# A fused two-block transformer forward on one core: modulation slabs in halves, output slabs split in place, gate order turned

## The reference, cut to what matters

```
mod   = silu(c) @ w_ada + b_ada                    # 6 x 1024 columns, 12 slabs of 512
h     = x * (1 + scale) + shift                    # slabs 0..3 give shift and scale
q, k, v, index, gb, gc, hc = split(h @ w_in)
attn  = softmax(mask_topk(rope(q) @ rope(k).T)) @ v
conv  = gb * short_conv(gc * hc)
mix   = concat(rms(attn), rms(conv)) @ w_out       # w_out: 2 slabs of 512 columns
x     = alpha * x + gate * mix;  then layer norm, SwiGLU, layer norm
```

```
h = h + swiglu(rms_norm(h, norm_ffn))
h = h + sigmoid(rms_norm(h, ple_norm) @ ple_w_gate) * (p @ ple_w_proj)
```

## Time and profile before

| | us |
|---|---|
| median of 3 runs | 1129.81 |
| lowest, highest | 1126.03, 1134.69 |
| the profiled execution | 1127.35 |
| its span in the profile | 1125.6 |

### The profile page before, as it was taken

One profiled execution on the slowest core, in us unless ns is written; L12 is line 12 of the kernel. 1 busy time (PEld: TensorE's weight loads), 2 busy tenths in 40 slices (PEclk: granted clock), 3 DMA queues, 4 the chain that ended last, 5 costly groups with the idle time before them and its releaser, 6 DMA issues.

```text
span 1125.6 us, 20288 instructions
## 1 busy us (share of the span) xinstructions
PE 1064.8 (95%) x7913; PEld 984.5 (87%) x7913; DVE 720.5 (64%) x1127; ACT 554.3 (49%) x954; POOL 223.8 (20%) x248
## 2 busy tenths in 40 slices
PE   5999988999999899989999999979987999999998
PEld 5577677999999698879999999978865899999998
DVE  4785777777645567748565645666768766564554
ACT  2223555544454666327454544655446764544453
POOL 0110002323312121012333311141110133332102
PEclk9999989999999999999999999989998999999999
DMA  9962464577557354404555456644440264645651
GB/s 351 400 266 75 150 237 138 168 248 265 153 157 223 103 205 142 159 1 143 191 191 180 147 155 191 225 150 150 150 150 1 76 225 160 212 133 148 202 191 39
DMA packets 183556, 192.78 MB, mean 171 GB/s; under 512 B 5881, under 2 KB 143394, under 8 KB 183490
## 3 DMA queue, kind: packets, MB, share of 16 engines
q1 hardware_dynamic: 182480, 191.15, 50.3%
q0 software_dynamic: 144, 0.52, 0.2%
q10 hardware_dynamic: 866, 0.21, 0.1%
HBM read 190.83 MB, written 1.05 MB: 170 GB/s over the span
## 4 chain that ended last, share of the span: by engine, by line
PE 56%; DVE 5%; ACT 2%; issue 2%; POOL 1%; POOLq 0%; ACTq 0%
PE gemm L1978 17%; PE gemm L1980 17%; PE gemm L1979 17%; PE aux L2438 1%; DVE wlo L1321 1%; PE aux L2100 1%; PE aux L2502 1%; ACT whi L867 1%; DVE state L1873 1%; PE aux L2496 1%; DVE neg_max L1937 1%; DVE d_p L1953 0%; DVE g_b L1827 0%; PE gemm L2528 0%; ACT ohi L1103 0%
## 5 line engine op out<-in xcount | busy, mean ns | idle before, releaser
L1321 DVE TENSOR_TENSOR wlo<-raw,whi 128x1024 fp32r<-128x1024 f32 (+2 forms) x324 | 369.1, 1184 | 78.7 <-ACT whi L867 78.2
L1978 PE MATMUL gemm<-ohi,whi 128*128 128x256 f32 x1376 | 388.7, 283 | 1.7 <-DVE wlo L1321 1.4
L1979 PE MATMUL gemm<-olo,whi 128*128 128x256 f32 x1376 | 385.6, 280 | 0.0
L1980 PE MATMUL gemm<-ohi,wlo 128*128 128x256 f32 x1376 | 384.5, 279 | 0.0
L867 ACT ACTIVATE whi<-raw 128x1024 fp32r<-128x1024 f32 (+2 forms) x324 | 288.7, 956 | 66.0 <-PE gemm L1980 50.9
L1978 PEld LDWEIGHTS gemm<-ohi,whi 128*128 128x128 f32 x1376 | 259.7, 189 | 5.1 <-issue 2.6
L1979 PEld LDWEIGHTS gemm<-olo,whi 128*128 128x128 f32 x1376 | 259.9, 189 | 0.6 <-issue 0.5
L1980 PEld LDWEIGHTS gemm<-ohi,wlo 128*128 128x128 f32 x1376 | 259.7, 189 | 0.0
L1980 PE MATMUL gemm<-acthi,wlo 128*128 128x256 f32 x528 | 147.8, 280 | 0.0
L1978 PE MATMUL gemm<-acthi,whi 128*128 128x256 f32 x528 | 147.5, 279 | 0.0
L1979 PE MATMUL gemm<-actlo,whi 128*128 128x256 f32 x528 | 147.3, 279 | 0.0
(11 more groups left out here) (351 smaller groups left out, 1509.5 us busy)
## 6 DMA issues: line engine op xcount, KB each, us to landing
raw<-in_ffn_w_in SPq DMA_DIRECT2D x44, 1024.0 KB, 6.2
raw<-in_ffn_w_out SPq DMA_DIRECT2D x32, 704.0 KB, 5.8
part<-in_w_ada SPq DMA_DIRECT2D x32, 512.0 KB, 10.5
raw<-in_gla_w_in SPq DMA_DIRECT2D x6, 2048.0 KB, 7.6
raw<-in_diff_w_in SPq DMA_DIRECT2D x6, 2048.0 KB, 7.6
raw<-in_w_gate SPq DMA_DIRECT2D x11, 1024.0 KB, 6.4
raw<-in_w_up SPq DMA_DIRECT2D x11, 1024.0 KB, 8.6
raw<-in_w_down SPq DMA_DIRECT2D x16, 704.0 KB, 5.4
```

What stands on the lines that cost most here:

```text
L1321: dve.tensor_tensor(wlo[hslot][:, q * w:(q + 1) * w], raw[slot][:, q * w:(q + 1) * w], whi[hslot][:, q * w:(q + 1) * w].bitcast(F32), ALU. ...
L1978: pe.matmul(dst, st_hi, mv_hi, start=start, stop=False)
L1979: pe.matmul(dst, st_hi, mv_lo, start=False, stop=False)
L1980: return pe.matmul(dst, st_lo, mv_hi, start=False, stop=stop_)
```

## The change

The first two modulation slabs leave the ring and come in two halves of four row blocks, each with its own semaphore, and the sums of the second stand on PE ahead of the transposes of x. The two slabs of w_out leave the ring as well: they are loaded into the place of `wlo` (`out_w`), ACT splits them from there, and DVE's low part overwrites them in place. Slab 0 is split beside the in_gc projection and made low ahead of the heads, slab 1 a quarter a head in heads 4 to 7. The modulation parts get ten buffers from the start, two of them are used earlier (parts 8 and 9 ahead of the heads, part 10 before the first maxima), and the list of parts by head ends with single ones. The group norms of attention tiles 0 and 1 move up into heads 6 and 7, and `out_columns` begins with these two row blocks ahead of the last product with v. In the gate projections the sigmoid's table is loaded by a small dummy instruction, the first sigmoid comes after one quarter, the sigmoid of a tile comes ahead of the operands of the tile before, DVE adds ahead of making the low operand, and slab 1's quarters are split one, one, one and one over tiles 0 to 2.

```diff
-    ada = lambda i: Phase(f"ada{i}", 1, SLAB, 0, 1, by="mod", ahead=False, ring=i < 2, slot=i % 2)
+    ada = lambda i: Phase(f"ada{i}", 1, SLAB, 0, 1, by="mod", ahead=False, ring=False, slot=i % 2)
...
-        Phase("out0", 2, SLAB, 4, 1, slot=1), *ffn(0),
+        Phase("out0", 2, SLAB, 4, 1, ring=False, slot=1), *ffn(0),
...
+        out_w = [sb(f"out_w{i}", SLAB, at=place[f"wlo{i}"]) for i in range(2)]
...
-            return (n % 8, n // 8) if n < 16 else (8 + n % 2, (n - 16) // 2)
+            return (n % 10, n // 10) if n < 18 else (8 + n % 2, 1 + (n - 18) // 2)
...
-        DONE_BEFORE = {"gate_up0": 4, "gate_up1": 2, "gate_up2": 2, "diff_q": 2}
+        DONE_BEFORE = {"out0": 4, "gate_up0": 4, "gate_up1": 2, "gate_up2": 2, "diff_q": 2}
...
+            elif first and ph.name in ("ple_gate1", "ple_gate2"):
+                each = (1, 0, 0, 0) if act else (0, 0, 0, 0)
...
+            if at.i == 0 and ph.name in ("ple_gate1", "ple_gate2"):
+                return {0: (1,) if act else (0, 1), 1: (2,), 2: (3,)}.get(t, ())
             return {0: (2,), 1: (3,)}.get(t, ()) if act else {0: (1,), 1: (2,), 2: (3,)}.get(t, ())
...
+            def load_out(i):
+                sp.wait_ge(*((tile_done, PH["in_q"].tile0 + 4), (part_used, 18))[i])
+                sp.dma_start(flat(out_w[i], KT, 512), kmaj(a["w_out"][0], 0, 512, i)).then_inc(out_in[i], 16)
...
             for t in range(4):
                 take("in_gc", t, tl(gc, t), gc_ready)
+                for q in {0: (0, 1), 2: (2, 3)}.get(t, ()):
+                    split(PH["out0"], At(0), q)
...
             def beside_head(i):
-                if i in (5, 6):
-                    act.wait_ge(part_used, 12)
-                    split_all("out0", None, range(2 * i - 10, 2 * i - 8))
                 if i == 5:
-                    group_squares(0, attn_ready, 2)
+                    group_root(0, G[0])
+                if i >= 4:
+                    split(PH["out0"], At(1), i - 4)
                 if i == 6:
-                    group_root(0, G[0])
                     group_squares(2, gated_ready, 2)
+                    high_parts(0, 1)
                 if i == 7:
-                    high_parts(0, 1)
                     group_root(2, G[1])
...
+                act.activation(lam[:, 6:7], eps[:, 0:1], ACT.Sigmoid)
...
+                    if k == 1 and m == KT - 1:
+                        operand(m - 1)
                     act.wait_ge(ple_in, n + 1)
                     wait(act, ple_prod, n - k)
                     act.activation(tl(sg, t % 2), tl(gt, t % 2), ACT.Sigmoid).then_inc(ple_sig, 1)
+                    if k == 1 and 0 < m < KT - 1:
+                        operand(m - 1)
                     for q in quarter_between(ph, at, t, act=True):
                         ahead(ph, at, q)
-                    if k == 1:
-                        act.wait_ge(ple_added, m + 1)
-                        scaled_high_and_square(m, B("norm_mix_2", KT + m), a0, dhi, gsq)
...
-            add_heads(range(0, 4))
             modulate_part(6)
             modulate_part(7)
+            add_heads(range(0, 4))
+            modulate_part(8)
+            modulate_part(9)
             add_heads(range(4, IH))
...
-            PARTS_OF_HEAD = ((8, 9), (10, 11), (12, 13), (14, 15), (16, 17), (18, 19), (20,), (21,))
+            PARTS_OF_HEAD = ((11, 12), (13, 14), (15, 16), (17, 18), (19, 20), (21,), (22,), (23,))
             me.again()
+            for q in range(4):
+                low(PH["out0"], At(0), q)
+            modulate_part(10)
             masked_maxima(0)
             for i in range(NH):
                 invert_sums(i)
                 if i + 1 < NH:
                     masked_maxima(i + 1)
+                if i == 6:
+                    mix_norm(0, 1)
+                if i == 7:
+                    mix_low(0, 1)
                 if i < 4:
                     short_conv(i)
                 else:
                     gated_conv(i - 4)
-                for q in {6: (0, 1), 7: (2, 3)}.get(i, ()):
-                    low(PH["out0"], At(0), q)
-                if i == 7:
-                    mix_norm(0, 1)
+                    low(PH["out0"], At(1), i - 4)
                 for n in PARTS_OF_HEAD[i]:
                     modulate_part(n)
...
                     me.did(dve.tensor_tensor(tl(gt, t % 2), bank[:, 0:T], rstd[:, 0:T], ALU.mult), ple_in)
+                    low_between(ph, at, t)
+                    add(m)
                     if k == 1 and m:
                         rest(m - 1)
-                    low_between(ph, at, t)
-                    add(m)
...
             last_columns(1)
+            first_sums_of(1)
             pe.wait_ge(x_in, 16)
...
-            out_columns(0, range(4), OUT_ORDER[0:4], True, False)
+            out_columns(0, range(4), OUT_ORDER[0:2], True, False)
+            values(NH - 1)
+            group_stats((3, 1), C("blk"), mix_sq, X[0:2])
+            out_columns(0, range(4), OUT_ORDER[2:4], False, False)
```

More of the change, by code:

```diff
@@ L532, in build @@
         sources = {
-            **{f"ada{i}": columns(ada, 512 * ADA_ORDER[i]) for i in range(2)},
             "in_gc": columns(w_in, C_GC), "in_hc": columns(w_in, C_HC), "in_gb": columns(w_in, C_GB),
-            "out0": columns(a["w_out"][0], 0),
             "gate_up0": gate_up(a["w_gate"][0], 0, a["w_up"][0], 0), "down0": down(a["w_down"][0]),
@@ L614, in load_ada @@
             def load_ada(n):
-                for half, (dst, src) in enumerate(ada_halves(n, early[n - 2])):
-                    sp.dma_start(dst, src).then_inc(early_in[n - 2][half], 16)
+                for half, (dst, src) in enumerate(ada_halves(n, raw[n] if n < 2 else early[n - 2])):
+                    sp.dma_start(dst, src).then_inc(early_in[n][half], 16)
+            def load_out(i):
+                sp.wait_ge(*((tile_done, PH["in_q"].tile0 + 4), (part_used, 18))[i])
+                sp.dma_start(flat(out_w[i], KT, 512), kmaj(a["w_out"][0], 0, 512, i)).then_inc(out_in[i], 16)
             def load_q():
@@ L634, in _ @@
                 if not ph.ring:
+                    for more in behind.get((ph.name, 0), ()):
+                        more()
                     continue
+                if ph.name in ("in_gc", "in_hc"):
+                    sp.wait_ge(mod_done, 1 + ph.slot)
                 def load(at, ph=ph):
@@ L864, in split @@
                 hslot = (ph.j0 + at.parity) % 2
-                if q == 0:
+                src = out_w[hslot] if ph.name == "out0" else raw[slot]
+                if q == 0 and ph.name == "out0":
+                    act.wait_ge(out_in[at.i], 16)
+                elif q == 0:
                     act.wait_ge(landed[slot], at.of(ph.landed))
-                act.activation(whi[hslot][:, q * w:(q + 1) * w], raw[slot][:, q * w:(q + 1) * w],
+                act.activation(whi[hslot][:, q * w:(q + 1) * w], src[:, q * w:(q + 1) * w],
                                ACT.Copy).then_inc(hi_ready, 1)
@@ L977, in gemm @@
                 rounds(act, ph, body)
-            def split_all(name, free=None, qs=range(4)):
-                if free:
-                    wait(act, tile_done, PH[free].tile0 + 4)
-                for q in qs:
-                    split(PH[name], At(0), q)
             def take(name, t, dst, ready):
@@ L1234, in ple, with operand @@
                 root(X[0], T, 1.0 / D, 1, rstd[:, 0:T])
+                act.activation(lam[:, 6:7], eps[:, 0:1], ACT.Sigmoid)
+                def operand(m):
+                    act.wait_ge(ple_added, m + 1)
+                    scaled_high_and_square(m, B("norm_mix_2", KT + m), a0, dhi, gsq)
                 def after(at, t):
@@ L1250, in ple @@
                 if k == 1:
+                    operand(KT - 1)
                     next_seen(scaled=True)
@@ L1380, in modulate @@
             def modulate(i):
-                src = raw[PH[f"ada{i}"].slot] if i < 2 else early[i - 2]
+                src = raw[i] if i < 2 else early[i - 2]
                 acc = macc0[i][:, :]
@@ L1385, in modulate @@
                 for k in range(last + 1):
-                    if i < 2 and k == 0:
-                        dve.wait_ge(landed[i], 16)
-                    if i >= 2 and k % 4 == 0:
-                        dve.wait_ge(early_in[i - 2][k // 4], 16)
+                    if k % 4 == 0:
+                        dve.wait_ge(early_in[i][k // 4], 16)
                     w, c = src[:, 512 * k:512 * (k + 1)], c_act[:, k:k + 1]
@@ L2116, in last_columns @@
                 src, i = raw[n], ADA_ORDER[n]
-                pe.wait_ge(landed[n], 16)
+                pe.wait_ge(early_in[n][1], 16)
                 for k in (KT - 2, KT - 1):
@@ L2286, in _ @@
                     values(i - 1)
[L2287 to L2290 removed]
+                if i in (0, 1, 3, 5):
+                    modulation({0: 5, 1: 6, 3: 7, 5: 8}[i])
                 if i == 6:
                     group_stats((2,), C("blk"), mix_sq, G[1:2])
[L2293 to L2294 removed]
             def next_operand():
```

45 lines of the change are left out of this document (22 added, 23 removed).

## The result

| | before | after |
|---|---|---|
| median, us | 1128.81 (13 runs) | 1136.80 (13 runs) |
| lowest, highest | 1125.59, 1134.69 | 1130.80, 1138.80 |
| ratio, with its 95% interval | | 1.0055 [1.0036, 1.0074] |
| profiled execution, span | 1127.35, 1125.6 | 1138.80, 1137.0 |

What follows compares the result with a forecast made beforehand. PE, busy 95% of the span, was taken as the bound, so time is won only where it waits or runs slower. Terms 0.9 - 0.3 + 0.9 + 1.5 = +3.0 us on 1127.35, plus 2.5 to the median: 1132.8 us; range 1121 to 1142.

Steps and rivals of the forecast that it cites:

- the term for heads and output projection: Heads to slab 1 and POOL's sums: -8.0 against +7.5, and +0.2 overrun, giving -0.3 us; ends -7.8 and +0.6.
- Start: First modulation slabs: DVE's wait goes, but slab 1's sums delay the transposes of x; +0.9 us, ends 0 and +1.7.
- Heads 0 to 4: Heads 0 to 3 keep two parts each as before; no gain was claimed here.
- Heads 4 and 5: ACT waits for w_out's slab 1, then a serial chain of quarters and parts; heads 7.5 us longer up to `rsum`(6).
- The rival in which the heads hide the slab: Slab 1's load or quarters fit beside other waits, so the 7.5 us don't come: 1125.3 us, chance 0.25.
- From `rsum`(6) to slab 1: Last heads and output projection: slab 0 finished at +27.4 instead of 33.6 after `rsum`(6), 6.2 us won.
- the sign of no PE wait over 1.5 us there: From head 7 to the end of slab 1, PE was to have no wait over 1.5 us.
- Layer norm: Behind slab 1, POOL's sums come 1.8 us earlier relative to PE; PE's wait for POOL under 2.5 us.
- First gate: First gate projection: PE stands 3.4 us for the fourth quarter, then a 3.45 us loop, half clock; +0.9, ends -3, +2.
- Second gate: Second gate projection: PE stands 1.5 us for the fourth quarter and everything behind moves; +1.5 us, ends 0 and +4.4.
- The lower clock takes over: Rival: PE's new idle stretches in head 5, tail and gates bring half clock; +6.7, 1139.5 us, chance 0.17.

Runs made afterwards that it cites:

- Early w_out: Changed kernel with buffers of modulation parts 10 to 13 and 14 to 17 swapped, so w_out's slab 1 loads sooner: ratio 1.0005 [0.9986, 1.0023].
- the earlier read: Changed kernel with DVE's modulation read ahead of the norms of tiles 6 and 7, slab 0's second half in two passes: ratio 1.0018 [0.9992, 1.0043].
- second mended kernel: Changed kernel with w_out's slab 1 loaded sooner, modulation read moved ahead, gates' new order kept, quarters at old places: 0.9921 [0.9900, 0.9941], 1121.74 us.
- heads alone: Kernel before with only the change to w_out, modulation parts, heads and output projection: ratio 1.0024 [1.0005, 1.0043], +2.7 us.
- Start alone: Kernel before with only the first two modulation slabs in halves, sums ahead of the transposes; run twice: 1.0007 [0.9993, 1.0022] and 1.0004 [0.9982, 1.0026].
- gate-only kernel: Kernel before with only the change to both gate projections: ratio 1.0030 [1.0007, 1.0053].
- undone: Changed kernel with both gate projections back in the old order (quarters, operands, low operand): ratio 1.0023 [1.0007, 1.0038].

## Why the prediction was right, and which of its steps were not

The forecast was +3.0 us, the ratio gives +6.2 [4.1, 8.4]: slower, inside the range of 1121 to 1142, within the 1% named as likeliest. The size is another matter: it is twice the forecast, which lies outside the interval, and a range of 21 us forgives that. The main part of what was missed is the term for heads and output projection, -0.3 against +2.7 measured.

**Start: right that it matters little.** `om` was foreseen at 26.8 and came at 26.35; the wait of 0.93 for DVE's first sum went with the halves, which the +0.9 had counted on; the sums of slab 0 began 1.25 earlier (13.24 instead of 14.49), and so the sums of slab 1 pushed the transposes by 0.44 only. Foreseen +0.9; two measurements give +0.5 and +0.8, with zero inside both.

**Heads 0 to 4: a gain that was not foreseen.** The prediction read two places of idleness or lower clock in the first 190 us. There are more: the kernel before also has a low stretch in head 2, by these windows for PE alone (stretch, length, PE busy, granted clock, DMA share, GB/s):

```profile
102.00:105.00 3.00, 3.00 (x17) 0.78 0.00 0
105.00:108.00 3.00, 3.00 (x10) 0.66 0.01 3
```

DVE then waits 2.1 us for the projection (3.8 in the second profile), and `rsum`(2) to `rsum`(3) takes 8.2 us or more in the five profiles with the old heads, 6.5 in the nine with the new ones, where the clock is at 1.00 there. That is 1.6 us won. It is also why the absolute time failed: `rsum`(6) was foreseen near 140.5 and came at 136.95.

**Heads 4 and 5: right, nearly to the number.** Foreseen: slab 1 issued 1.56 us ahead of `rsum`(4), landing at +6.1, ACT waiting 3 to 4 us, `rsum`(5) at +11.5 and `rsum`(6) at +18.9. Measured: 1.58 ahead, +6.1, 3.74, +11.2 and +18.4. Early w_out took the wait away and 3.9 us of the 11.2 with it. The rival in which the heads hide the slab is refuted by its own test: ACT's quarter began 3.7 us late.

**From `rsum`(6) to slab 1: this step failed.** I had the end of slab 0 at +27.4 instead of 33.6, a gain of 6.2 (its 0.117 us for a matmul is a twenty-fourth of a tile's 2.83 us, not a quarter as written). Slab 1 began at +33.5 and +32.2 in the two profiles (+34.0 and +34.4 before, by the same mark). Three things stood in its place, in the first profile: the last product with v ended 2.5 us late, since the clock was at half for the projection that DVE needed (its wait of 3.29) behind PE's waits in heads 4 and 5; 2.3 for the bank that the modulation's read holds, a claim that stood in the code (`banks.claim(X[3], mod_read)`) and that I had not followed into DVE's order, so the sign of no PE wait over 1.5 us there failed too; and 1.7 at the lower clock behind that wait; 0.4 was won elsewhere. The experiments show each: with early w_out slab 1 begins at +31.0, with the earlier read at +29.5, with both at +26.9, and at +28.6 in the second mended kernel, whose clock fell once more in the last heads. So the foreseen +27.4 can be had, and the steps named are what stood in its way. Up to gate_up0 the first pair then adds up: -0.4 at the start, -1.7 in heads 0 to 4, +7.0 in heads 4 and 5, -0.5 from `rsum`(6) to slab 1, -2.2 from there, together +2.2. The sum for heads and output projection was -0.3 with an upper end of 0.6; heads alone measured +2.7 [0.6, 4.9].

**Layer norm: right** that POOL's sums come earlier relative to PE (1.8 foreseen, 2.0 measured), and that gain stays. The longer wait for DVE's low operand ahead of gate_up0 (1.78 instead of 0.27) costs nothing: from the norm's first sums to gate_up0 it takes 7.17 us, before 7.36. DVE's low operand is what ends it in both; before, PE filled more of it at its lower clock. Start alone, which keeps the old output projection, had the same wait of 1.76 in its first profile, with 7.15 us.

**First gate: the stall right, what follows it only in its sum.** Foreseen 3.4 us, measured 3.47; the loop 3.45, measured 3.44. The half clock that I put behind the stall was absent in the changed kernel's first profile (granted 1.00 to the end of the gate) and came behind the gate, in diff_q, instead. In the gate-only kernel and in the second profile it was where foreseen and hidden by POOL's and DVE's loop. Up to the squares of d_sq the changed kernel took 45.9 and 45.8 us where the kernel before took 44.6 twice: +1.3 and +1.1, against +0.9. That this is so near is luck: the kernel with the gate change alone has the same stall and takes 44.4. It lacks a fall in diff_q that the four other profiles with the stall have (1.7 us lost; 45.6 to 46.0 us).

**Second gate: right.** Stall 1.5 foreseen, 1.57 measured; the stretch to the last transposes 26.7 us instead of 24.8, +1.8 against +1.5. By ratios both gates together cost +3.4 (alone) and +3.6 (undone), with intervals of 2 to 3 us to each side; the prediction's +2.4 lies inside.

**The lower clock takes over: not the main thing, yet a part of it.** There are more falls in the first profile of the changed kernel than of the other, and fewer in its second. The prediction had one fall at the gate and one less in the tail; what it missed is that PE's two waits of 1.2 and 2.7 us in heads 4 and 5 bring a stretch of about 10 us near half clock, in each profile that has them (5.1 us lost), for which the sum had nothing and this rival 0.9. It shows in the time as the 2.5 us of the last product with v. The Trainium skill (TensorE: Matmul & The Clock Gate, Why this matters for your kernels) says that idle gaps cost the higher clock; the trace agrees, and with early w_out, which takes the waits away, that stretch is at 1.00.

## What to carry to other kernels

Where a slab is split beside running work, its last quarter has a due time (here four tiles), and any reordering that puts another step of the loop ahead of it should be counted against that time first; keeping the quarters where they were removed the stall and kept the shorter loop. Where a buffer is shared by parts of a stream and a later load, give the load the place of the parts that are used first. Before a gain is put down for a reordered tail, follow every claim of a bank in it to the instruction that releases it, in that engine's new order.

## What the runs showed of the hardware that was not expected

Two executions of one kernel agree to 0.1 us in most of their long waits (2.65 and 2.64, 2.29 and 2.28, 3.47 and 3.38, 1.57 and 1.64), and differ in part in where TensorE is granted its lower clock: 17.7 and 22.9 us lost in the kernel before, 23.6 and 17.0 in the changed one. A wait beside such a fall moves with it: the one for slab 1's low quarter, in the kernel before, was 0.28 and 1.49 us. One pair of profiles is therefore good for durations and most waits, and not for a difference of a few us in the end. A wait of PE need not be followed by a fall at once: behind 3.47 us of waiting the clock was 1.00 for over 15 us in one profile of the changed kernel, and in four other profiles with the same wait it fell within 5 us.
